# Layers written out, SwiGLU blocks of 4, 6, 6, 6 tiles, and x turned tile by tile

## The reference

```
for l in range(DEPTH):                                    # DEPTH = 2
    n = rms_norm(x, attn_norm[l])
    h = n @ w_in[l]                                       # 1024 -> 1472 columns
    o_a = sliding-window attention with sinks (8 q heads, 2 kv heads)
    o_b = latent attention (4 heads, absorbed form)
    x = x + concat(rms_norm(o_a), rms_norm(o_b)) @ w_out[l]
    n = rms_norm(x, ffn_norm[l])
    x = x + (silu(n @ w_gate[l]) * (n @ w_up[l])) @ w_down[l]     # 1024 -> 2816 -> 1024
return rms_norm(x, final_norm), new keys, values and latents of both layers
```

## Time and profile before

| | us |
|---|---|
| median of three runs | 1614.78 (1612.4 to 1615.67) |
| the profiled execution | 1614.81 |
| its span, first to last instruction | 1613.5 |
| PE busy | 1480.8 (92%) |
| DVE busy | 951.4 (59%) |
| ACT busy | 663.5 (41%) |
| POOL busy | 177.0 (11%) |
| mean granted clock of TensorE | 0.960 |

### The profile page before, as it was taken

The page is one execution under the profiler, slowest core; times in us unless marked ns, Lnnn a source line. Parts: engine busy times, 40 slices in busy tenths (PEclk is TensorE's granted clock), DMA queues, the critical chain, the costliest instruction groups (busy, mean ns, idle before and its releaser), DMA issues.

```text
span 1613.5 us, 26565 instructions
## 1 busy us (share of the span) xinstructions
PE 1480.8 (92%) x9510; PEld 1388.9 (86%) x9510; DVE 951.4 (59%) x1582; ACT 663.5 (41%) x1292; POOL 177.0 (11%) x121
## 2 busy tenths in 40 slices
PE   3997778899999999999989777889999999999997
PEld 3877666799899999999968666668999999999997
DVE  5257545476955846746633864446587476475565
ACT  2255535433423523524425463353244244253344
POOL 5123300220000000000110440021200000000004
PEclk7997989899999999999999988998999999999999
DMA  3222012023232232321123201131314223133112
GB/s 130 77 91 69 14 47 62 27 79 92 61 111 67 84 95 63 95 82 53 51 78 96 71 27 40 28 81 40 105 40 119 59 79 108 57 99 92 60 41 104
DMA packets 150633, 116.01 MB, mean 72 GB/s; under 512 B 14656, under 2 KB 142912, under 8 KB 150464
## 3 DMA queue, kind: packets, MB, share of 16 engines
q1 hardware_dynamic: 150496, 114.23, 23.5%
HBM read 109.43 MB, written 6.62 MB: 72 GB/s over the span
## 4 chain that ended last, share of the span: by engine, by line
PE 69%; DVE 12%; issue 9%; ACT 6%; POOL 3%; DMA 1%; SPq 0%; DVEq 0%; ACTq 0%; POOLq 0%
PE ps L523 25%; PE ps L1086 9%; PE ps L1085 9%; PE ps L1084 9%; PE ps L568 2%; PE ps L570 2%; PE ps L569 2%; ACT whi L1149 1%; POOL pwx L2178 1%; POOL pw L2178 1%; DVE wlo L1593 1%; PE ps L882 1%; PE ps L908 1%; PE ps L795 1%; DVE xT L2093 1%
## 5 line engine op out<-in xcount | busy, mean ns | idle before, releaser
L1593 DVE TENSOR_TENSOR wlo<-wraw,whi 128x1024 fp32r<-128x1024 f32 (+2 forms) x120 | 136.6, 1139 | 227.9 <-ACT whi L1149 227.9
L1149 ACT ACTIVATE whi<-wraw 128x1024 fp32r<-128x1024 f32 (+2 forms) x120 | 108.9, 915 | 272.0 <-PE ps L523 179.9
L1084 PE MATMUL ps<-tth,ringh 128*128 128x320 f32 x576 | 176.8, 307 | 3.1 <-ACT k L1497 1.8
L1086 PE MATMUL ps<-tth,ringl 128*128 128x320 f32 x576 | 178.0, 309 | 0.0
L1085 PE MATMUL ps<-tl,ringh 128*128 128x320 f32 x576 | 177.3, 308 | 0.0
L523 PE MATMUL ps<-hh,whi 128*128 128x320 f32 x704 | 161.3, 310 | 4.5 <-DVE wlo L1593 2.8
L523 PE MATMUL ps<-hh,wlo 128*128 128x320 f32 x704 | 160.4, 309 | 0.0
L523 PE MATMUL ps<-hl,whi 128*128 128x320 f32 x704 | 160.3, 309 | 0.0
L1084 PE MATMUL ps<-tbh,ringh 128*128 128x320 f32 x432 | 133.6, 309 | 1.9 <-DVE ringl L1978 1.9
L1085 PE MATMUL ps<-tbl,ringh 128*128 128x320 f32 x432 | 133.5, 309 | 0.0
L1086 PE MATMUL ps<-tbh,ringl 128*128 128x320 f32 x432 | 133.5, 309 | 0.0
(11 more groups left out here) (370 smaller groups left out, 3355.4 us busy)
## 6 DMA issues: line engine op xcount, KB each, us to landing
raw_gate<-w_gate SPq DMA_DIRECT2D x18, 1024.0 KB, 5.4
raw_up<-w_up SPq DMA_DIRECT2D x18, 1024.0 KB, 5.4
wraw<-w_down SPq DMA_DIRECT2D x48, 384.0 KB, 3.3
wraw<-w_in SPq DMA_DIRECT2D x16, 512.0 KB, 3.6
wraw<-w_out SPq DMA_DIRECT2D x32, 128.0 KB, 2.9
wraw<-w_out SPq DMA_DIRECT2D x16, 256.0 KB, 3.0
wraw<-w_gate SPq DMA_DIRECT2D x8, 512.0 KB, 3.9
wraw<-w_up SPq DMA_DIRECT2D x8, 512.0 KB, 3.8
```

What stands on the lines that cost most here:

```text
L1084: mm(o, wh[:, c, :], xh[:, c, :], start=fresh and c == 0, stop=False, skip_group_check=True)
L1086: ins = mm(o, wl[:, c, :], xh[:, c, :], start=False, stop=c == KH - 1, skip_group_check=True)
L1149: run(whi[:, slot(s, unit_width(u))], wraw[:, slot(s, unit_width(u))], ACT.Copy).then_inc(unit_hi.sem, 1)
L1593: vec.tensor_tensor(wlo[:, w], wraw[:, w], whi[:, w], ALU.subtract).then_inc(unit_lo.sem, 1)
```

## The change

1. The hardware loop over layers is gone: each engine's list is written out twice with constant semaphore values. Unit 0 of layer 1 is split at the end of layer 0's list: on ACT behind the last `normed`, on DVE ahead of the last add to `xT`.
2. x is turned token tile by token tile as each lands (8 blocks of a tile, ACT copies the lower four chunks to `xT`, DVE the upper four). Then ACT makes `nh` and the square of each chunk with `normed`, DVE the low halves; units 0 and 1 are split behind chunks 0 and 3. GpSimd only adds the squares. The mask is loaded behind unit 1 and cast after the low halves.
3. The SwiGLU blocks are 4, 6, 6, 6 tiles: block 0 is the four plain tiles alone with a down projection of its own, the 18 groups follow in blocks of six. The steps of the right operands are spread over the plain tiles and block 0's down projection in another order. The load of the first pair of `w_up` tiles stands behind two down units.

The rest of the diff renames semaphores and shifts their starting values.

```diff
-TILES = [6, 6, 6, 4]
+TILES = [4, 6, 6, 6]
...
-TILE0 = [0, 6, 12, 18]
+TILE0 = [0, 4, 10, 16]
...
-GROUPS_OF = [(0, 2), (2, 8), (8, 14), (14, 18)]
+GROUPS_OF = [(0, 0), (0, 6), (6, 12), (12, 18)]
...
-DOWN_PAIR = [3, 0, 1, 2, 0, 1, 2, 3]
+DOWN_PAIR = [[0, 1, 2, 3, 0, 1, 2, 3]] + 3 * [[3, 0, 1, 2, 0, 1, 2, 3]]
...
-    def layers(eng):
-        with eng.Fori(0, DEPTH) as layer:
-            yield layer
+    def row_slot(tile):
+
+        return tile if tile < PLAIN else (tile - PLAIN) % 6
...
     def _(sp):
         sp.dma_start(kc[:, :], a["consts"][:, 0:K_W]).then_inc(consts_in.sem, 16)
         sp.dma_start(gv[:, G_NEXT:G_NEXT + NC_], a["consts"][:, K_GAIN:K_GAIN + NC_]).then_inc(consts_in.sem, 16)
-        sp.dma_start(mask_in[:, :], a["consts"][:, K_W:]).then_inc(consts_in.sem, 16)
         for t in range(TS):
-            sp.dma_start(xin[:, t, :], a["x_prompt"][0, tok(t), :]).then_inc(x_in.sem, 16)
-        sp.dma_start(xin[:, TS, :], a["x_sample"].rearrange("b s d -> (b s) d")).then_inc(x_in.sem, 16)
+            sp.dma_start(xin[:, t, :], a["x_prompt"][0, tok(t), :]).then_inc(tile_in[t].sem, 16)
+        sp.dma_start(xin[:, TS, :], a["x_sample"].rearrange("b s d -> (b s) d")).then_inc(tile_in[TS].sem, 16)
...
-        for l in layers(sp):
+        for l in range(DEPTH):
...
                 if u == 1:
-
+                    if l == 0:
+                        sp.dma_start(mask_in[:, :], a["consts"][:, K_W:]).then_inc(win_in.sem, 16)
                     sp.wait_ge(n_lo.sem, n_lo.at(l, 1))
                     sp.dma_start(gv[:, 0:G_KV], a["vectors"][l][:, 0:G_KV]).then_inc(vectors_in.sem, 16)
...
-            load_pair(1)
             for blk in range(NBLK):
                 first, end = GROUPS_OF[blk]
                 load_down(blk, 0)
                 load_down(blk, 1)
+                if blk == 0:
+                    load_pair(1)
...
-        pe.wait_ge(consts_in.sem, 48)
-        pe.wait_ge(x_in.sem, 16 * NT)
-        for c in range(NC_):
-            if c >= 4:
-                pe.wait_ge(x_new.sem, c - 3)
-            for t in range(NT):
-                bank = 2 * (c % 4) + t // 4
-                ins = turn(ps[:, bank, (t % 4) * P:(t % 4 + 1) * P], xin[:, t, c * P:(c + 1) * P], ident)
+        pe.wait_ge(consts_in.sem, 32)
+        for t in range(NT):
+            pe.wait_ge(tile_in[t].sem, 16)
+            if t >= 4:
+                pe.wait_ge(x_act.sem, t - 3)
+                pe.wait_ge(x_new.sem, t - 3)
+            for c in range(NC_):
+                ins = turn(ps[:, 2 * (t % 4) + c // 4, (c % 4) * P:(c % 4 + 1) * P], xin[:, t, c * P:(c + 1) * P], ident)
             ins.then_inc(tile_turned.sem, 1)
-        for l in layers(pe):
+        pe.wait_ge(x_act.sem, NT)
+        pe.wait_ge(x_new.sem, NT)
+        for l in range(DEPTH):
...
-                    b0 = 2 * DOWN_PAIR[d]
+                    b0 = 2 * DOWN_PAIR[blk][d]
                     pe.wait_ge(unit_lo.sem, unit_lo.at(l, u + 1))
-                    if d == 0 and blk >= 1:
+                    if blk == 0 and d < 4:
+                        pe.wait_ge(scaled.sem, scaled.at(l, 2 * PLAIN - 2 if d < 2 else 2 * PLAIN + d - 3))
+                    elif d == 0:
                         pe.wait_ge(x_new.sem, x_new.at(l, 8 + 8 * blk))
...
-        act.wait_ge(consts_in.sem, 48)
+        act.wait_ge(consts_in.sem, 32)
+        for t in range(NT):
+            act.wait_ge(tile_turned.sem, t + 1)
+            run(xT[:, 0:4, tok(t)], ps[:, 2 * (t % 4), :].rearrange("p (c n) -> p c n", c=4), ACT.Copy).then_inc(x_act.sem, 1)
+        act.wait_ge(x_act.sem, NT)
+        act.wait_ge(x_new.sem, NT)
         for c in range(NC_ - 1):
-            act.wait_ge(tile_turned.sem, c + 1)
-            turned = ps[:, 2 * (c % 4):2 * (c % 4) + 2, :].rearrange("p a n -> p (a n)")[:, 0:T]
-            run(nh[:, c, :], turned, ACT.Copy, scale=gv[:, G_NEXT + c:G_NEXT + c + 1]).then_inc(n_hi.sem, 1)
-        for l in layers(act):
+            normed(0, c, xT, gv[:, G_NEXT + c:G_NEXT + c + 1], nh, n_hi, adds_before(c))
+            if c == 0:
+                weight_hi(0, 0)
+            if c == 3:
+                weight_hi(0, 1)
+        for l in range(DEPTH):
 
 
             last = NC_ - 1
-            weight_hi(l, 0)
+            if l > 0:
+                weight_hi(l, 0)
             act.wait_ge(x_new.sem, x_new.at(l, 0))
             run(nh[:, last, :], xT[:, last, :], ACT.Copy, scale=gv[:, G_NEXT + last:G_NEXT + last + 1]).then_inc(n_hi.sem, 1)
-            weight_hi(l, 1)
+            if l > 0:
+                weight_hi(l, 1)
...
             for i in range(PLAIN):
                 odd, u = i % 2, U_FFN + 2 * i
-                if i + 1 < PLAIN:
-                    weight_hi(l, u + 2)
+                weight_hi(l, u + 2)
                 if i == 0:
                     act.wait_ge(stat_sum.sem, stat_sum.at(l, 4))
                     run(sd[:, 0:NT], ps[:, 7, 500:505], ACT.Sqrt, bias=eps, scale=1.0 / D).then_inc(stat_sd.sem, 1)
                     spread_out(3, ps[:, 4:6, :])
-                if 1 <= i <= 2:
-                    right_high_plain(i)
                 act.wait_ge(scaled.sem, scaled.at(l, 2 * i + 1))
                 run(tg[:, odd, :], tg[:, odd, :], ACT.Silu).then_inc(silu_new.sem, 1)
                 if i == 0:
                     right_high_plain(0)
-                if i <= 2:
-                    right_high_sums(i)
-                if i == PLAIN - 1:
-                    for x in (1, 5, 6):
-                        left_high(0, x)
+                if i >= 2:
+                    right_high_sums(i - 1)
                 act.wait_ge(h_new.sem, h_new.at(l, i + 1))
-                if i + 1 < PLAIN:
-                    weight_hi(l, u + 3)
+                weight_hi(l, u + 3)
                 run(hh[:, i, :], tu[:, odd, :], ACT.Copy).then_inc(h_hi.sem, 1)
-                if i == 2:
-                    right_high_plain(3)
-                    right_high_sums(3)
-            left_high(0, 3)
+                if i == 0:
+                    right_high_sums(0)
+                else:
+                    right_high_plain(i)
...
                     u = U_DOWN + blk * NC_ + d
                     if d + 2 < NC_:
                         weight_hi(l, u + 2)
+                    if blk == 0 and d == 0:
+                        right_high_sums(3)
                     if 2 <= d < 2 + len(following):
...
-        dve.wait_ge(consts_in.sem, 48)
+        dve.wait_ge(consts_in.sem, 32)
+        for t in range(NT):
+            dve.wait_ge(tile_turned.sem, t + 1)
+            vec.tensor_copy(xT[:, 4:8, tok(t)], ps[:, 2 * (t % 4) + 1, :].rearrange("p (c n) -> p c n", c=4)).then_inc(x_new.sem, 1)
+        dve.wait_ge(x_new.sem, NT)
+        for c in range(NC_ - 1):
+            dve.wait_ge(n_hi.sem, c + 1)
+            low(nl[:, c, :], xT[:, c, :], gv[:, G_NEXT + c:G_NEXT + c + 1], nh[:, c, :]).then_inc(n_lo.sem, 1)
+            if c == 0:
+                weight_lo(0, 0)
+            if c == 3:
+                weight_lo(0, 1)
+        dve.wait_ge(win_in.sem, 16)
         vec.tensor_copy(kmask[:, :], mask_in[:, :])
...
-        for c in range(NC_):
-            if c < NC_ - 1:
-                dve.wait_ge(n_hi.sem, c + 1)
-            else:
-                dve.wait_ge(tile_turned.sem, NC_)
-            turned = ps[:, 2 * (c % 4):2 * (c % 4) + 2, :].rearrange("p a n -> p (a n)")[:, 0:T]
-            vec.tensor_copy(xT[:, c, :], turned).then_inc(x_new.sem, 1)
-            if c < NC_ - 1:
-                dve.wait_ge(x_new.sem, c + 1)
-                low(nl[:, c, :], xT[:, c, :], gv[:, G_NEXT + c:G_NEXT + c + 1], nh[:, c, :]).then_inc(n_lo.sem, 1)
-        for l in layers(dve):
+        for l in range(DEPTH):
...
             last = NC_ - 1
-            weight_lo(l, 0)
             dve.wait_ge(n_hi.sem, n_hi.at(l, 1))
             low(nl[:, last, :], xT[:, last, :], gv[:, G_NEXT + last:G_NEXT + last + 1], nh[:, last, :]).then_inc(n_lo.sem, 1)
-            weight_lo(l, 1)
+            if l > 0:
+                weight_lo(l, 1)
...
             for i in range(PLAIN):
                 odd, u, base = i % 2, U_FFN + 2 * i, 4 * (i % 2)
-                if i + 1 < PLAIN:
-                    weight_lo(l, u + 2)
+                weight_lo(l, u + 2)
                 if i >= 1:
                     hidden_lo(i - 1, tu[:, 1 - odd, :])
                 if i == 0:
                 vec.tensor_tensor(halves(tg[:, odd, :]), ps[:, base:base + 2, 0:HALF], halves(rA[:, :]), ALU.mult).then_inc(scaled.sem, 1)
                 if i == 0:
                     right_rows(0)
-                    right_sums(0)
                 elif i == 1:
...
+                    right_low_plain(0)
+                    right_low_sums(0)
+                else:
+                    right_sums(i - 1)
+                    right_low_plain(i - 1)
                 dve.wait_ge(unit_used.sem, unit_used.at(l, u + 2))
```

(51 more changed lines are left out.)

49 lines of the change are left out of this document (18 added, 31 removed).

## The result

The changed kernel takes 1588.62 us (median of four runs, 1587.84 to 1590.1) against 1613.59 us (four runs) of the kernel before: a ratio of 0.9835, 95% interval 0.9819 to 0.985. The forecast was 1593.0. The profiled executions stand 27.0 us apart, and that is the difference explained here. First the page of the changed kernel: span, busy time by engine, and the chain that ended last.

A forecast was written before the change was run, and what follows sets the result against it. The prediction took TensorE as the bound, busy 92% of the span and 69% of the chain. Its terms, 8.4 + 8.4 + 4.5 - 1.6 + 1.1 + 1 = 21.8 us, off 1614.81 gave 1593.0 us, range 1582 to 1604.

The forecast's parts named there:

- The start: Layer 0 up to its third weight unit: earlier first matmul, then about 4 us idle and a cold unit; 8.4 us gained.
- The layer step: Layer 0 to layer 1: the 6.29 us of idle TensorE and the cold clock go; 8.4 us gained.
- The last block: Last SwiGLU block, both layers: six tiles per down unit cover the chain, all waits go; 4.5 us gained.
- The first block: First SwiGLU block: old waits of 4.2 us a layer end, new ones of 5.0 begin; -1.6 us in both layers.
- Tail and registers: Last add no longer behind, 1.1 us gained; register instructions of the loop's waits end, 1 us gained.
- Rival B: First block's new waits don't appear, or register work was on attention's path: 9 us more gain, 1584; chance 0.14.
- C: First block goes cold: 2.8 us idle halves the clock, 3.4 us lost twice, 1600; chance 0.14.
- D: Layer step isn't closed, the next layer's first weights' split or load being late: 6 us less gain, 1599; chance 0.09.
- E: Slower: every down unit of the first block waits for VectorE; at 5.4 us per unit 30 us lost, 1623; chance 0.05.
- the four outcomes called faster: Whole kernel: forecast 0.56, B 0.14, C 0.14 and D 0.09, all lower than 1614.8; faster was given 0.92.

The follow-up runs named there:

- the written-out kernel: The kernel before with its two layers written out and nothing else: 1606.64 us against 1615.19, ratio 0.9939.
- the second session: A later session in which the changed kernel was executed once more without edit: 1584.52 us, against 1588.62 in the first.
- The late low half: The changed kernel, but VectorE makes the low half of the first block's last tile five times over in each layer: 1594.47 us.

## Why the prediction was right, and where its terms were off

The stages moved as forecast but for the first block, and the sum came out 5 us too small: the start gave 1.9 less than its term, the last blocks 2.1 more, the first blocks 4.7 more, the rest together 0.2 more. That the start's miss covered a part of the others is luck.

**The start (8.4, measured 6.52).** The path was right: an early first matmul, then idle time ahead of unit 2, whose load stands behind the last low half, then a unit that gives 2.0 us back to the clock. The step that was mis-sized is VectorE's list: I took 1.6 times its undisturbed time, and the last low half ended at 34.0 instead of 32, with the weight split at 2.0 times and the cast at 3.5. The run without GpSimd's adds shows the cause. The sum as written, 15.7 + 1.6 x 9.3, gives only 30.6; the 31.5 to 32.5 has a us or two on top for which the text names no row. TensorE stood idle 7.7 us instead of 4: unit 2 came 1.9 us later than forecast, and the first matmul 1.3 us earlier.

**The layer step (8.4, measured 8.34).** Right in size; the two runs that take it apart show 2.9 us for writing out and 2.1 for the split's place. The slack that I gave the split was 0.4 us; the trace has none, the first matmul starts 0.10 us behind the split's end, since that split too ran beside GpSimd (1.83 us instead of 1.23). The Trainium skill's rule on taken branches ("Runtime: NRT & Kernel Launch", section Instruction fetch mechanics) fits the written-out kernel, in which ScalarE's 1.65 us of waiting are gone; that run can't tell them from the loaded table, which went with them.

**The last block (2.25 a layer, measured 3.3).** The mechanism held, all waits went. The step that was mis-sized is the price of a wait: I added up idle times, 0.89 + 0.73 + 0.65 = 2.27. The matched matmuls lost 1.05, 0.89 and 0.82 at those places, 0.16 us more per wait: a matmul takes 0.31 us and the next starts 0.147 behind it, and a matmul that waits gives up that overlap. The second matmul behind each wait starts another 0.10 to 0.11 us late (in the rows above, a pair behind a wait takes 0.56 us where others take 0.46). The other 0.24 us are a fourth wait, too short to show as idle time: with it the sum is 3.31.

**The first block (-0.8 a layer, measured +1.55).** This is the term with the wrong sign, and the largest miss: 4.7 us over the two layers. The three waits are those of the prediction in place, cause and order, and none came later. Two steps were off. The larger is again the price of the waits that ended: taken as 4.2 us of idle time, while the same matmuls lost 5.6, so 1.4 us a layer. That alone turns the sign. The other is the new waits, reckoned at 5.0 us and costing 4.1: as idle time they were 1.8, 0.9 and 0.6 instead of 2.8, 1.2 and 1.0. Most of this is "I find it still 1.5 us from its `tu`". VectorE's list between two plain tiles was summed at 14.2 us against 14.1, but its `tu` operations follow each other in 13.4, 13.3 and 13.9 us, so it catches up: the last `tu` starts at 420.75, 0.7 us after the first down matmul at 420.07. That takes 0.8 us from the first wait. The other two hang on steps behind the same `hl` and so don't move with it; the lost overlap of 0.16 us, which the idle time leaves out, is about half of what they were smaller by.

**Tail and registers (2.1).** The tail's 1.1 us came as forecast (1.07). For register work 1 us was taken; outside the two places where the clock differs, the attention stretches show some 1 us in both layers together, with a scatter as large. (The 1.2 us that writing out gained in the plain tiles and first blocks belong to the first block's term.) Rival B's 9 us are not there.

**The rivals.** B's time of 1584 was met by the second session's 1584.5, but by luck: the waits of the first block did appear, and the register work is not 9 us. C didn't happen: the idle time was 1.8 us instead of 2.8. The late low half shows that the clock does fall after 5.2, at 2.6 us a layer instead of the 3.4 assumed, and that the later waits absorb 1.8 of it. Whether 2.8 us would have been enough in this stretch no run shows. D and E did not happen; against D there was no slack left. The chances of the four outcomes called faster add up to 0.93, not 0.92.

## What to carry to other kernels

When an engine is made to start early, look at once for the next thing on its path: here the idle time ahead of the third unit and the half clock behind it took back 9.6 of the 16.1 us that the early start had won, and moving two loads from behind an unrelated wait gave 6.7 us. Compare two traces of the same work by matched instructions and by stages, not by totals: here the short stages of dense matmuls repeat to 0.01 us, the long ones to 0.6, the sparse ones vary by 3, and an effect of 2 us in the one is invisible in a total that holds the other. Before a sparse stage is put down to an edit, compare its granted clock over the same matmuls. And price a wait, removed or new, by what the matched instructions lose at it: here 0.26 us more than its idle time.

## What the runs showed of the hardware

The granted clock in the attention stretches isn't a property of the code: the same program had 0.83 and 0.91 over the same 203 matmuls, which took 40.02 and 36.99 us, the attention stretches differed by 1.5 and 2.7 us, and the medians of the two sessions by 4.1. And GpSimd's adds slow VectorE's operations unequally: beside them a 128 x 1024 subtraction took 2.52 us instead of 1.23, a 128 x 768 cast 1.92 instead of 0.55, and a low half of 128 x 640 up to 2.1 instead of 0.9.
